# Rows of cumulated decays spread over the partitions: one fp32r product of three terms in the place of fp32 products with short contractions

## The reference

```python
# second block, ssd mixer: 32 heads in 8 groups, 64 channels a head
acum = jnp.cumsum(ac, axis=1)
seg = acum[:, :, None] - acum[:, None, :]
lmat = jnp.exp(jnp.where(causal[None, :, :, None, None], seg, -jnp.inf))
cb = jnp.einsum('btgn,bsgn->btsg', cc, bc)
y_diag = jnp.einsum('btsg,btsgr,bsgrp->btgrp', cb, lmat, xdt)

# third block, forgetting attention: 16 heads of 64
cum = jnp.cumsum(jax.nn.log_sigmoid(f_logit.astype(jnp.float32)), axis=1).transpose(0, 2, 1)
sc = jnp.einsum("bhqd,bhkd->bhqk", q[:, :, qs:qe], k[:, :, :qe]).astype(jnp.float32) * scale
sc = sc + cum[:, :, qs:qe, None] - cum[:, :, None, :qe]
sc = jnp.where(allowed, sc, -jnp.inf)
p = jax.nn.softmax(sc, axis=-1)
```

## Time and profile before

| | |
|---|---|
| median of 3 runs | 3240.32 us (3228.05 to 3245.45) |
| profiled execution: its own time | 3242.05 us |
| its span | 3240.2 us |
| PE busy in the span | 3032.1 us (94%) |
| PE weight loads | 2750.8 us (85%) |
| DVE busy | 1922.8 us (59%) |
| ACT busy | 1563.1 us (48%) |
| DMA, share of 16 engines by queue 1 | 44.7% |
| mean granted clock of TensorE | 0.95 of full speed |

### The profile page before, as it was taken

How to read it: one execution, slowest core, us unless ns; L and a number is a source line. 1 busy time by engine, 2 the same in 40 slices (tenths; PEclk the granted TensorE clock), 3 DMA queues, 4 the chain that set the end, 5 groups by cost and what they waited for, 6 DMA issues and landing times.

```text
span 3240.2 us, 47088 instructions
## 1 busy us (share of the span) xinstructions
PE 3032.1 (94%) x19662; PEld 2750.8 (85%) x19662; DVE 1922.8 (59%) x3098; ACT 1563.1 (48%) x2449; POOL 157.8 (5%) x211
## 2 busy tenths in 40 slices
PE   8999898799879969999999999997999999899998
PEld 8978897799769858798888999996788889789896
DVE  4555555555665455767345898449655564535675
ACT  4444444444444444465244444449445545444563
POOL 0000000000000001000000000009000000000000
PEclk9999999999889989999689999999999999889999
DMA  6544454355325535244035445540455553424453
GB/s 202 194 138 163 156 189 166 130 183 201 103 91 184 191 121 197 91 146 149 28 90 195 157 157 182 182 169 1 164 191 193 207 190 113 133 63 161 147 190 141
DMA packets 304227, 489.91 MB, mean 151 GB/s; under 512 B 10816, under 2 KB 236480, under 8 KB 295312
## 3 DMA queue, kind: packets, MB, share of 16 engines
q1 hardware_dynamic: 302880, 479.50, 44.7%
q0 software_dynamic: 1136, 7.41, 0.6%
HBM read 484.77 MB, written 2.10 MB: 150 GB/s over the span
## 4 chain that ended last, share of the span: by engine, by line
PE 84%; DVE 10%; ACT 3%; issue 2%; POOL 1%; DMA 0%; SPq 0%; DVEq 0%; POOLq 0%; ACTq 0%
PE ps L418 29%; PE ps L391 15%; PE ps L387 14%; PE ps L388 14%; PE ps L851 2%; DVE halves L1079 2%; PE ps L369 1%; DVE AR L1131 1%; ACT AR L2084 1%; PE ps L761 1%; PE ps L870 1%; DVE AR L1726 1%; POOL st L968 1%; PE ps L892 1%; DVE AR L1724 1%
## 5 line engine op out<-in xcount | busy, mean ns | idle before, releaser
L2055 ACT ACTIVATE halves<-raw 128x1024 fp32r<-128x1024 f32 (+2 forms) x907 | 947.8, 1051 | 997.6 <-PE ps L391 527.8
L1079 DVE TENSOR_TENSOR halves<-raw,halves 128x1024 fp32r<-128x1024 f32 (+2 forms) x907 | 1085.8, 1214 | 486.6 <-ACT halves L2055 482.4
L387 PE MATMUL ps<-XH,halves 128*128 128x256 f32 x3968 | 1001.9, 289 | 3.0 <-issue 2.2
L388 PE MATMUL ps<-XL,halves 128*128 128x256 f32 x3968 | 994.0, 287 | 0.0
L387 PEld LDWEIGHTS ps<-XH,halves 128*128 128x128 f32 x3968 | 775.8, 196 | 7.0 <-issue 3.4
L388 PEld LDWEIGHTS ps<-XL,halves 128*128 128x128 f32 x3968 | 775.6, 195 | 1.1
L391 PE MATMUL ps<-XH,halves 128*128 128x256 f32 x3968 | 564.8, 285 | 30.1 <-DVE halves L1079 30.1
L391 PEld LDWEIGHTS ps<-XH,halves 128*128 128x128 f32 x3968 | 515.0, 193 | 37.4 <-DVE halves L1079 36.5
L418 PE MATMUL ps<-halves,R 128*128 128x512 f32 x1872 | 433.2, 393 | 9.1 <-DVE R L1095 7.2
L418 PEld LDWEIGHTS ps<-halves,R 128*128 128x128 f32 x1872 | 354.9, 190 | 84.3 <-issue 8.1
L418 PE MATMUL ps<-halves,XH 128*128 128x512 f32 x1600 | 406.1, 393 | 5.7 <-DVE halves L1079 3.3
(11 more groups left out here) (326 smaller groups left out, 2597.1 us busy)
## 6 DMA issues: line engine op xcount, KB each, us to landing
raw<-in_w_ffn_in SPq DMA_DIRECT2D x88, 1024.0 KB, 5.0
raw<-in_w_in SPq DMA_DIRECT2D x74, 1024.0 KB, 5.3
raw<-in_uT SPq DMA_DIRECT2D x64, 1024.0 KB, 4.8
raw<-in_peer_v SPq DMA_DIRECT2D x64, 1024.0 KB, 4.8
raw<-in_w_ffn_out SPq DMA_DIRECT2D x44, 1024.0 KB, 4.8
raw<-in_w_up SPq DMA_DIRECT2D x24, 1024.0 KB, 5.7
raw<-in_mlstm_w_in SPq DMA_DIRECT2D x12, 1024.0 KB, 5.3
raw<-in_w_down SPq DMA_DIRECT2D x12, 1024.0 KB, 4.9
```

What stands on the lines that cost most here:

```text
L387: mm(o, hi[:, q, 0:M], xh[:, k0 + q, :], start=first and q == 0, stop=False)
L388: mm(o, hi[:, q, 0:M], xl[:, k0 + q, :], start=False, stop=False)
L1079: te.tensor_tensor(lo, src, hi.bitcast(F32), ALU.subtract).then_inc(k.lo_made, 1)
L2055: act(hi, src, ACT.Copy).then_inc(k.hi_made, 1)
```

## The change

The rows are made in three copies, on partitions 0 to 95: the 32 (twice the 16) weight columns of the logits stand three (six) times in new inputs `w_dt` and `w_fo`, and so do the constants `dtb`, `al` and `fo`. A new helper, `in_three`, splits a row into three fp32r terms, whose sum is the row: the first 32 partitions hold the first term, the next 32 the second, the last 32 the third. A selector `sel` (fp32r, 128x48, with the identity three times below each other and, in columns 32 to 47, less it) is made once at the start. `decay` then makes one fp32r product with contraction 96 over all 384 columns, and the two mask products. `score` makes one such product for the keys over 384 columns, and for each part one for the queries, one for the mask and the fp32 product of queries and keys, in another order.

```diff
-    ("lam", 10, 128), ("bi", 1, 4), ("bf", 1, 4), ("dtb", 1, 32), ("al", 1, 32), ("fo", 1, 16),
+    ("lam", 10, 128), ("bi", 1, 4), ("bf", 1, 4), ("dtb", 1, 96), ("al", 1, 96), ("fo", 1, 96),
...
-    small(w, 9216, 1, 32)
+    small(d["w_dt"], 0, 1, 96)
...
-    small(w, 5632, 1, 16)
+    small(d["w_fo"], 0, 1, 96)
...
         def decay(h):
             b = aux.take(pe, ("m2", "L", h))
-            sel = bc(ident[0:32, h:h + 1], [32, 128])
-            mm(ps[:, b, 0:256], sel, ac, start=True, stop=False)
-            mm(ps[:, b, 0:256], identb[:], mkq2, start=False, stop=True)
-            mm(ps[:, b, 256:384], sel, ac[:, 128:256], start=True, stop=False)
+            pe.wait_ge(*s["vec"].need("m2.acx"))
+            mm(ps[:, b, 0:384], bc(k.sel[0:96, h:h + 1], [96, 128]), acx, start=True, stop=False)
+            mm(ps[:, b, 0:256], identb[:], mkq2, start=False, stop=False)
             ins = mm(ps[:, b, 256:384], identb[:], mkq, start=False, stop=True)
...
-            sl = ident[0:16, h:h + 1]
+            sel, less = k.sel[0:96, h:h + 1], k.sel[0:96, 32 + h:33 + h]
             pe.wait_ge(*main.gone(("m3.k", 6)))
-            pe.wait_ge(*s["vec"].need("m3.rows"))
-
-            def part(o, n, q0):
-                mm(ps[:, b, o:o + n], qT[p0:p0 + 64, h // 2, q0:q0 + 128],
-                   kT[p0:p0 + 64, h // 2, 0:n], start=True, stop=False)
-                mm(ps[:, b, o:o + n], bc(sl, [16, 128]), ncum[:, 0:n], start=False, stop=False)
-                mm(ps[:, b, o:o + n], cumr[:, q0:q0 + 128], bc(sl, [16, n]), start=False, stop=False)
-                return mm(ps[:, b, o:o + n], identb[:], mqk2 if n == 256 else mqk, start=False, stop=True)
-
-            part(0, 128, 0)
-            filled(("m3", "s", h), part(128, 256, 128))
+            pe.wait_ge(*s["vec"].need("m3.cx"))
+            mm(ps[:, b, 0:384], bc(less, [96, 128]), cx, start=True, stop=False)
+            for o, n, q0 in ((0, 128, 0), (128, 256, 128)):
+                mm(ps[:, b, o:o + n], cx[:, 128 + q0:256 + q0], bc(sel, [96, n]), start=False, stop=False)
+                mm(ps[:, b, o:o + n], identb[:], mqk2 if n == 256 else mqk, start=False, stop=False)
+                ins = mm(ps[:, b, o:o + n], qT[p0:p0 + 64, h // 2, q0:q0 + 128], kT[p0:p0 + 64, h // 2, 0:n],
+                         start=False, stop=n == 256)
+            filled(("m3", "s", h), ins)
...
+    def in_three(dst, src):
+
+        low = [slice(g, g + 32) for g in (32, 64)]
+        chained(te.tensor_copy(dst, src))
+        for g in low:
+            chained(te.tensor_tensor(src[g], src[g], dst[g].bitcast(F32), ALU.subtract))
+        for g in low:
+            chained(te.tensor_copy(dst[g], src[g]))
+        chained(te.tensor_tensor(src[low[1]], src[low[1]], dst[low[1]].bitcast(F32), ALU.subtract))
+        chained(te.tensor_copy(dst[low[1]], src[low[1]]))
...
             te.tensor_tensor_scan(ac, ones, e_, 0.0, ALU.mult, ALU.add).then_inc(*step.mark("m2.rows"))
-            for _ in range(3):
-                yield
+            yield
+            acx = k.part_at(26112, 384)[0:96, :]
+            v.wait_ge(*step.need("m2.rows"))
+            in_three(acx[:, 0:256], ac)
+            yield
+            te.tensor_copy(acx[:, 256:384], acx[:, 128:256].bitcast(F32)).then_inc(*step.mark("m2.acx"))
+            yield
...
             chained(te.tensor_tensor_scan(cumr, ones, cum, 0.0, ALU.mult, ALU.add))
-            te.tensor_scalar(ncum, cumr, -1.0, None, ALU.mult).then_inc(*step.mark("m3.rows"))
+            in_three(cx[:, 128:384], cumr)
+            te.tensor_copy(cx[:, 0:128], cx[:, 128:256].bitcast(F32)).then_inc(*step.mark("m3.cx"))
...
     te.tensor_copy(k.identb[:], k.ident[:])
+    for g in (0, 32, 64):
+        te.tensor_copy(k.sel[g:g + 32, 0:32], k.ident[g:g + 32, g:g + 32])
+        te.tensor_scalar(k.sel[g:g + 32, 32:48], k.ident[g:g + 32, g:g + 16], -1.0, None, ALU.mult)
```

More of the change, by code:

```diff
@@ L269, in __init__ @@
         (self.raw, self.halves, self.AR, self.part_at, XH, XL, self.XF, self.cols, self.ident,
-         self.identb, self.iota, self.mask, self.st, self.xsel, self.ps, self.spill) = mem
+         self.identb, self.sel, self.iota, self.mask, self.st, self.xsel, self.ps, self.spill) = mem
         self.X = (XH, XL)
@@ L713, in mix2 @@
         rw = [k.AR[0:32, 23552 + 256 * i:23808 + 256 * i] for i in range(6)]
-        dt, ac = rw[0], rw[5]
-        small("m2", 1, 32, rx)
+        dt, ac, acx = rw[0], rw[5], k.part_at(26112, 384)[0:96, :]
+        small("m2", 1, 96, rx)
         def dt_cols():
@@ L872, in mix3 @@
                 filled(("m3.rg", f, i), ins)
-        small("m3", 1, 16, rx)
+        small("m3", 1, 96, rx)
         qT, kT, vv = k.ar(17536, 8, 256), k.ar(19584, 8, 256), k.ar(21632, 2, 1024)
-        rw = [k.AR[0:16, 25216 + 256 * i:25472 + 256 * i] for i in range(5)]
-        cumr, ncum = rw[2], rw[3]
+        cx = k.part_at(26240, 384)[0:96, :]
         features("m3.q", 8, X, rx)
@@ L1558, in mix2 @@
         xs, xd, tmpc = k.ar(4096, 2, 2048), k.ar(8192, 2, 2048), k.ar(15360, 6, 256)
-        rw = [k.AR[0:32, 23552 + 256 * i:23808 + 256 * i] for i in range(6)]
+        rw = [k.AR[0:96, 23552 + 256 * i:23808 + 256 * i] for i in range(6)]
         dt, e_, r0, r1, ones, ac = rw
@@ L1564, in mix2 @@
         v.wait_ge(*main.gone(("m2.ya", 6)))
-        te.tensor_scalar(dt, ps[0:32, main.of(("m2", "small")), 0:256], col("dtb"), None, ALU.add) \
+        te.tensor_scalar(dt, ps[0:96, main.of(("m2", "small")), 0:256], col("dtb"), None, ALU.add) \
             .then_inc(*main.done(("m2", "small")))
@@ L1575, in dt_rows @@
             v.wait_ge(*s["act"].need("m2.al"))
-            chained(te.tensor_scalar(cc[0:32, 255:256], cc[0:32, 255:256], -1.0, None, ALU.mult))
-            chained(te.tensor_scalar(e_, dt, cc[0:32, 255:256], None, ALU.mult))
+            chained(te.tensor_scalar(cc[0:96, 255:256], cc[0:96, 255:256], -1.0, None, ALU.mult))
+            chained(te.tensor_scalar(e_, dt, cc[0:96, 255:256], None, ALU.mult))
             yield
@@ L1858, in mix3 @@
         features(nothing, "m3.ga", 10)
-        rw = [k.AR[0:16, 25216 + 256 * i:25472 + 256 * i] for i in range(5)]
-        cum, e_, cumr, ncum, ones = rw
+        rw = [k.AR[0:96, 25216 + 256 * i:25472 + 256 * i] for i in range(4)]
+        cum, e_, cumr, ones = rw
+        cx = k.part_at(26240, 384)[0:96, :]
         weights()
         v.wait_ge(*full["m3", "small"])
-        te.tensor_scalar(cum, ps[0:16, main.of(("m3", "small")), 0:256], col("fo"), None, ALU.add) \
+        te.tensor_scalar(cum, ps[0:96, main.of(("m3", "small")), 0:256], col("fo"), None, ALU.add) \
             .then_inc(*main.done(("m3", "small")))
@@ L1868, in cum_rows @@
             yield
-            yield from log1p(e_, cumr, ncum)
+            yield from log1p(e_, cumr, ones)
             yield
@@ L2365, in dt_rows @@
                 yield
-            act(cc[0:32, 255:256], col("al"), ACT.Exp).then_inc(*s["act"].mark("m2.al"))
+            act(cc[0:96, 255:256], col("al"), ACT.Exp).then_inc(*s["act"].mark("m2.al"))
             yield
@@ L2536, in mix3 @@
         qT, kT, vv = k.ar(17536, 8, 256), k.ar(19584, 8, 256), k.ar(21632, 2, 1024)
-        rw = [k.AR[0:16, 25216 + 256 * i:25472 + 256 * i] for i in range(5)]
-        cum, e_ = rw[0], rw[1]
+        rw = [k.AR[0:96, 25216 + 256 * i:25472 + 256 * i] for i in range(2)]
+        cum, e_ = rw
         weights()
@@ L2725, in memory @@
     return (raw, halves, AR, part_at, XH[:], XL[:], XF, sb("cols", [128, NCOL]),
-            sb("ident", [128, 128]), sb("identb", [128, 128], BF16), sb("iota", [128, 128]),
+            sb("ident", [128, 128]), sb("identb", [128, 128], BF16), sb("sel", [128, 48], F32R), sb("iota", [128, 128]),
             sb("mask", [128, 384], BF16), sb("st", [128, 96]), sb("xsel", [128, 768]),
@@ L2773 @@
         "lam": tiles(z["lru_lambda_3"]), "bi": z["mlstm_b_gates"][0, :4, None],
-        "bf": z["mlstm_b_gates"][0, 4:, None], "dtb": z["dt_bias_2"].T, "al": z["a_log_2"].T,
-        "fo": z["b_forget_3"].T,
+        "bf": z["mlstm_b_gates"][0, 4:, None], "dtb": np.tile(z["dt_bias_2"].T, (3, 1)),
+        "al": np.tile(z["a_log_2"].T, (3, 1)),
+        "fo": np.tile(z["b_forget_3"].T, (6, 1)),
     }
@@ L2788 @@
         z["p"][:, 0].transpose(0, 2, 1).reshape(2, 2, 128, 256).transpose(0, 2, 1, 3))
+    arrays["w_dt"] = np.ascontiguousarray(np.tile(z["w_in_2"][0][:, 9216:9248], (1, 3)))
+    arrays["w_fo"] = np.ascontiguousarray(np.tile(z["w_in_3"][0][:, 5632:5648], (1, 6)))
     arrays["keys"] = np.ascontiguousarray(
```

## The result

| | before | after |
|---|---|---|
| median | 3240.28 us (3228.05 to 3245.45, 4 runs) | 3147.32 us (3146.22 to 3147.92, 4 runs) |
| ratio after / before | | 0.9718, 95% interval 0.9691 to 0.9745 |
| span of the profiled execution | 3240.2 us | 3145.3 us |
| mean granted clock | 0.95 | 0.968 |
| first `cb` to last `sums`, mixer | 137.3 us (1514.6 to 1651.9) | 75.0 us (1515.4 to 1590.4) |

The kernel is faster by 93 us; the forecast was 82 less (3158 us, range 3133 to 3194). The span of the profiled execution lost 94.9 us: 62.3 + 33.5 in the two stretches where the changed products run, and 0.8 the other way ahead of them. What lies between the two stretches took the same time. The profiled execution of the kernel before (3242.05 us) is one of its slower ones: four later sets of its runs have medians of 3229 to 3234 us.

The account below looks back on a forecast made before the run. TensorE, busy 94% of the span, was taken to bound the kernel. Gains 51.2 + 4.5 + 30.6 less costs 2.5 + 1.0 net 82.8 us: 3242.05 to 3159, median 1.7 lower, 3158 us; range 3133 to 3194.

Parts of the forecast that it names:

- the two stretches: Ssd mixer's body (118.2 us, clock 0.63) and attention of `mix3` (131.6 us, 0.87), both TensorE's: gains 51.2 and 30.6 us.
- The new decay: Mixer's body: one fp32r product and two masks take 0.50 us (0.35 to 0.64) at full clock, where 1.41 were.
- the low end: Decay of 0.35 us if 96 rows need no drain; the body would be 3.7 us shorter than at 0.50.
- The clock: TensorE's mean clock rises with the share of wide products: to 0.80 in the body, 0.95 in the attention.
- full clock: Rival: clock is full in both body and attention, gaining 101.3 us, 3139 us; chance 0.20.
- The rival of an unchanged clock: Clock stays 0.63 in the body and 0.87 in the attention: 55.5 us gained, 3185 us; chance 0.19.
- Group 0 and 1: Mixer: TensorE's 2.45 us wait for VectorE's copy of `cb` grows but ends earlier, gaining 4.5 us (0 to 4.9).
- The new score: Attention of `mix3`: a score takes 1.85 us, not 3.01; 1.16 less for each of 16 heads, 18.6 us.
- VectorE in `mix3`: The added three-term split puts 2.5 us on the path, where TensorE already waits 11.3 us for low halves.
- ScalarE's pace: Rival: in the mixer ScalarE's 0.84 us a head paces decays through the banks, 8.5 us back, 3167 us; chance 0.08.
- slower: Rival: clock falls to its low level in body and attention and stays: 3288 us; chance 0.03.
- no single pass: Rival: the new product isn't single-pass, a decay 1.31 us, a score some 3.2: 3240 us; chance 0.03.

Follow-up runs that it names:

- e10: Changed kernel with each decay as two fp32 products of 256 and 128 columns, 96 rows, a mask behind each: 3163.28 us, ratio 0.9792.
- e11: As e1, with one more fp32 product of 128 columns and 96 rows ahead in each decay, overwritten by the next: 3165.52 us, ratio 0.979.
- e2: Changed kernel with the decay's one product in fp32 and contraction 32, leaving out two of three terms: 3184.62 us, ratio 0.9852.
- e6: Changed kernel with VectorE's four large multiplications moved from behind group 0's decays to behind the convolutions of features 22 to 28: 3139.00 us, ratio 0.9708.
- e8: Changed kernel with the three-term split and 128-column copy of `mix3` done by GpSimd instead of VectorE: 3142.62 us, ratio 0.9715.
- e4: Only the ssd mixer's part of the change; rows and score in `mix3` as in the kernel before: 3167.44 us, ratio 0.9809.
- e5_control: Also called the control: the changed kernel itself, measured again beside three follow-up kernels: 3149.22 us, ratio 0.9733; the kernel before had 3233.83 beside it.
- e3: Changed kernel with contraction 32 in the decays' fp32r product, leaving out the two lower terms: 3152.56 us, ratio 0.9753.
- e1: Changed kernel with the decay's one product of 96 rows and 384 columns read as fp32, two passes: 3165.32 us, ratio 0.9792.
- e12: As e3, with the fp32r product of 32 rows issued four times in each decay, each overwriting the last: 3208.55 us, ratio 0.9888.

## Why the prediction was right

**Right as to place and as to work; right as to the clock's direction, but not for the reason given.** The gain is TensorE's, in the two stretches it named, and partly work and partly clock. Shorter work: 32 decays by 1.00 and 16 scores by 1.14, 50.2 us. The wait took back 6.9 (9.3 for 2.45). The rest of the 95.8 gained in the two stretches, 52.5 us, is by this count the clock: more than half. It is a difference of two executions, and the one before was a slow one.

**The new decay** was put at 0.50 and is 0.41, within 0.35 to 0.64. The product's step is 0.26, and 0.17, as estimated from the columns, only in the first decay behind a weight piece; the masks' steps are 0.12 and 0.03: they do shrink to their columns with 96 rows ahead of them. The prediction let this be the change of data kind or the change of rows; e10 shows that the rows make nearly all of it. The Trainium skill, "TensorEngine Tiling (Array Packing)", Key Properties, has the rule that a change of tiling mode drains TensorE. The runs agree if 32 rows are such a mode, with 0.12 to 0.13 us a change, and the low end that this rule gave was the nearer one.

**The clock** was the mis-sized term: 0.80 forecast in the body and 0.91 measured, 0.95 in the attention and 1.00. The body came to 58.7 us for 67.0, the attention to 98.0 for 101.0. The 0.80 was a pick between two ends, and the step that led to it doesn't hold: the forecast took the clock from the share of wide products, a quarter before and 36% after, whatever the rows of the others. e11 has as much side work as e2 and keeps 1.00. By the forecast's own count it has 0.82 + 4 x 1.09 + 2.4 = 7.6 us of side work to a piece of 2.9, so wide pieces have a share of 28%, near the quarter of before. The loss went with the 32-row products, and all of it, not part of it. That left only the stretch behind the wait at the low level. The rival "full clock" (3139 us) had this and missed by 8 us on the other side: it had no wait that keeps the body's first 12 us low.

**The rival of an unchanged clock** fell. The Trainium skill, "TensorE: Matmul & The Clock Gate", section "A second HAM failure mode: psum-queue depth-cycling", says that short idles between groups of products, as banks are cycled, make the clock swing, and so spoke for it. Here the banks cycle faster than before and the clock is 1.00 from 1544 on; in this kernel the cycling of banks alone did not lower it.

**Group 0 and 1.** The wait grew, as said, and ended 2.2 us earlier in the trace, 3.0 after the 0.8 by which everything had shifted, for 4.5. Unsaid was the price of a growing wait: 8.75 us of idle and a low clock behind it. e6 got 10.2 us of it back.

**The new score** was put at 1.85 and is 1.87. **VectorE in `mix3`** was put at 2.5: its operations take 2.77 us from 2673.67 to 2676.44, TensorE's waits grew by 2.2 and the way to the score by 3.4, of which the control shows only 1.2, the rest being the clock of that one execution. e8 takes the waits away again and gains 0.8 on the way. So the cost was 1 us or so and not the whole 2.5. In `mix2` the added operations cost at most the 0.8 us of the shift, as forecast (0). **ScalarE's pace, slower, and no single pass** did not come: 0.2 us of wait, and one record for each product of three terms.

**The model's smaller terms.** It priced a product of `sums` at 0.197 us, from `values`. In the trace after, the twelve of a group take 2.68 us (1561.61 to 1564.29) and not 2.4, and a `cb` pair 0.63 and not 0.82. That these were off hardly shows: 2.5 us more and 1.1 less in the body.

**The sum** by stretch: the mixer's side work gained 62.3 for 55.7 and the attention 33.5 for 30.6. The 3.5 of costs came as 3.4 ahead of the score, but as much was gained elsewhere between the stretches, where nothing was forecast. With the 0.8 that is 94.9 for 82.8: 6.6 and 2.9 from the stretches, by the clock and the shorter decay, and 3.5 less of cost, less the 0.8. Not all of it need be the change's: 9 us in the attention e4 gained with the old score. Against the same kernel before, run beside it in e5_control, the gain is 85 us; that this is so near the forecast is in part luck, since the clock was put too low and the execution that it started from was a slow one.

## What to carry to other kernels

- Small contractions among full-height products can cost twice: here 0.12 us at every change between 32 rows and 96 or 128, and, in decays of 1.11 us and more, the clock. Filling the idle rows (here with two more terms of the same number) is worth it even where the passes stay as they are: e10, still fp32 and still two products, has 50.7 of the 62.3 us that the mixer's side work gained.
- A low clock under a TensorE that is busy throughout should be traced to the products in it, their rows above all, before it is modelled as a share. And once the bound work shrinks, the next wait grows: move what it waits for in the same change.
- Group products by height and kind inside a step: it gave 0.35 us a score for a change of order.

## What was not expected of the hardware

- Behind a mask product of 128 rows, a product of 384 columns with 32 rows has a step of 0.37 us in fp32r and 0.84 in fp32 (e3, e2), one with 96 rows 0.26 and 0.70 (after, e1).
- Two fp32 products of 256 and 128 columns with masks between take 0.88 us at 96 rows, one of 384 takes 0.87: two more changes of data kind cost 0.01 us. Yet the fp32r product of 96 rows has 0.26 us behind a mask and 0.17 behind a weight piece; why is open.
- The granted clock was 0.63 under products that left TensorE no idle time (e12, 95 us busy of 95), and 1.00 under decays about as long of 96 rows (e11, 60 us busy of 60).
- GpSimd's cast of 96x256 to fp32r took 5.25 us, VectorE's 0.29; the subtractions on 32 rows took GpSimd 0.73 and VectorE 0.42.
